# Score pairs inside dense weight units, fp32 units by token tile, gate columns on column quarters: one change to a fused two-block kernel

## The reference

```python
# first block
h = rms_norm(x, mix_norm_pre)
q, kc, vc, ksl, vsl, kw, vw, gt, pin, u, v = split(h @ w_in)      # 512, 6 x 128, 24, 256, 256, 256
gates = sigmoid(gt)                       # 8 heads x 3 branches
kc, vc = compress(kc), compress(vc)       # 15 compressed keys/values per group (2 groups of 4 heads)
# per 128-token block: three masked softmaxes (compressed, selected, window keys), each
#   gates[..., b] * (softmax(q k^T * 64**-0.5 + rel_bias) v)
x = x + rms_norm(concat(attention, pool_mixer(pin), sgu_mixer(u, v)) @ w_out)
x = x + rms_norm(memory_attention(rms_norm(x), rms_norm(mem), w_mq, w_mk, w_mv, w_mo))
x = x + rms_norm(conv_ffn(rms_norm(x), w_up, w_down))
# second block
proj = rms_norm(x) @ w_in_2               # qkv 1536, z 512, a 4, b 4, c_q, c_kv, k_idx, w_idx 4, ug 512
x = x + concat(gdn_mixer(...), dsa_mixer(...), conv_mixer(...)) @ w_out_2
x = x + cross_attention(rms_norm(x), mem_2)
x = x + relu(rms_norm(x) @ mlp_w1)**2 @ mlp_w2
```

## Time and profile before

| | |
|---|---|
| runs | 885.93 us median, 885.88 to 888.56 (n = 3) |
| profiled execution | 883.95 us, span 882.0 us |
| TensorE (PE) busy | 841.3 us, 95% |
| VectorE (DVE) busy | 558.8 us, 63% |
| ScalarE (ACT) busy | 406.0 us, 46% |
| granted TensorE clock, mean | 0.986 of full |
| DMA | 135.83 MB, 154 GB/s |

### The profile page before, as it was taken

One profiled execution on the slowest core, in us unless ns is written; L12 is line 12 of the kernel. 1 busy time (PEld: TensorE's weight loads), 2 busy tenths in 40 slices (PEclk: granted clock), 3 DMA queues, 4 the chain that ended last, 5 costly groups with the idle time before them and its releaser, 6 DMA issues.

```text
span 882.0 us, 14015 instructions
## 1 busy us (share of the span) xinstructions
PE 841.3 (95%) x5884; PEld 748.5 (85%) x5884; DVE 558.8 (63%) x808; ACT 406.0 (46%) x555; POOL 125.2 (14%) x163
## 2 busy tenths in 40 slices
PE   5998999999989999999999999999889899999998
PEld 5996877799879999999958898888668799999996
DVE  4448866628267876776675979974665665555552
ACT  4358442463235545544343565454434454444440
POOL 1134000210020000000021979510000000000000
PEclk9996999999999999999999899999999999999999
DMA  8974345362426655455414514201214196555521
GB/s 278 326 214 168 125 140 167 127 232 96 143 72 237 238 193 192 162 193 198 165 48 146 181 60 146 94 3 49 95 48 143 48 313 216 188 190 191 190 97 48
DMA packets 92346, 135.83 MB, mean 154 GB/s; under 512 B 4435, under 2 KB 76763, under 8 KB 92156
## 3 DMA queue, kind: packets, MB, share of 16 engines
q1 hardware_dynamic: 90428, 129.68, 44.2%
q0 software_dynamic: 736, 2.63, 0.9%
q10 hardware_dynamic: 1120, 2.62, 0.9%
HBM read 133.34 MB, written 1.06 MB: 152 GB/s over the span
## 4 chain that ended last, share of the span: by engine, by line
PE 82%; DVE 10%; ACT 3%; DMA 2%; issue 2%; POOL 1%; SPq 0%; POOLq 0%; DVEq 0%; ACTq 0%
PE work L2115 39%; PE acc L2115 24%; PE work L2071 2%; PE work L2092 2%; DVE split_extra_slot L1407 2%; PE work L2722 1%; PE work L2060 1%; DVE split_operands L1407 1%; DMA weight_ring<-in_w_up 1%; ACT hT L913 1%; PE work L2077 1%; PE work L2403 1%; DVE x_normed L1561 1%; PE work L2286 1%; PE work L2422 1%
## 5 line engine op out<-in xcount | busy, mean ns | idle before, releaser
L1407 DVE TENSOR_TENSOR split_operands<-weight_ring,split_operands 128x2048 fp32r<-128x2048 f32 x74 | 170.3, 2304 | 104.5 <-ACT split_operands L933 104.2
L2115 PE MATMUL work<-split_operands 128*128 128x256 f32 x1872 | 230.5, 284 | 1.3 <-DVE split_operands L1407 1.2
L2115 PEld LDWEIGHTS work<-split_operands 128*128 128x128 f32 x1872 | 227.6, 192 | 4.3 <-issue 3.1
L2115 PE MATMUL acc<-split_operands 128*128 128x512 f32 x840 | 197.5, 391 | 2.7 <-DVE split_operands L1534 1.4
L933 ACT ACTIVATE split_operands<-weight_ring 128x2048 fp32r<-128x2048 f32 x74 | 141.2, 1911 | 114.2 <-PE acc L2115 46.2
L2115 PEld LDWEIGHTS acc<-split_operands 128*128 128x128 f32 x840 | 156.0, 188 | 35.4 <-issue 2.3
L2115 PE MATMUL work<-split_operands,split_extra_slot 128*128 128x256 f32 x1056 | 131.8, 284 | 2.2 <-DVE split_extra_slot L1407 1.6
L2115 PEld LDWEIGHTS work<-split_operands,split_extra_slot 128*128 128x128 f32 x1056 | 129.1, 192 | 4.0 <-issue 2.3
L1407 DVE TENSOR_TENSOR split_extra_slot<-weight_ring,split_extra_slot 128x2048 fp32r<-128x2048 f32 x34 | 78.5, 2309 | 28.0 <-ACT split_extra_slot L933 27.7
L920 ACT ACTIVATE arena<-work 128x512 f32<-128x512 f32 (+1 forms) x65 | 35.7, 551 | 114.3 <-PE work L2115 76.7
L933 ACT ACTIVATE split_extra_slot<-weight_ring 128x2048 fp32r<-128x2048 f32 x34 | 64.8, 1907 | 26.2 <-PE acc L2115 11.6
(11 more groups left out here) (321 smaller groups left out, 899.3 us busy)
## 6 DMA issues: line engine op xcount, KB each, us to landing
weight_ring<-in_mlp_w SPq DMA_DIRECT2D x32, 1024.0 KB, 5.3
weight_ring<-in_w_up SPq DMA_DIRECT2D x22, 1024.0 KB, 5.1
weight_ring<-in_w_in SPq DMA_DIRECT2D x20, 1024.0 KB, 6.2
weight_ring<-in_w_down SPq DMA_DIRECT2D x11, 1024.0 KB, 4.9
weight_ring<-in_w_out SPq DMA_DIRECT2D x8, 1024.0 KB, 4.9
weight_ring<-in_w_mk SPq DMA_DIRECT2D x4, 1024.0 KB, 5.4
weight_ring<-in_w_mv SPq DMA_DIRECT2D x4, 1024.0 KB, 5.5
weight_ring<-in_w_mq SPq DMA_DIRECT2D x4, 1024.0 KB, 5.1
```

The source lines that it names most:

```text
L1407: dve.tensor_tensor(slot[:, 1, :], weights(split_units[i], 2048), slot[:, 0, :], ALU.subtract).then_inc(low_ready, 1)
L2115: ins = pe.matmul(out, lhs(p), rhs(q), start=(start and n == 0), stop=(stop and n == 2))
```

## The change

1. **Scores.** The 16 head scores leave the 4 work banks for the 4 acc banks. Four pairs of heads of t=0 and four of t=1 are issued two before `u`, two inside `u`, two inside `v`, two inside `mk 0` (after 5 and 11 of the unit's 16 steps). The transposes of the memory rows and the compression move ahead of `v`, and `cmp_h` inside it; the compressed scores come after `mk 0` and `mk 1`. VectorE's and ScalarE's orders follow. The split memory rows' high part lies in `xn` now, and the places of the input units are `(extra, 20480, 8704, extra, 20480, extra, 20480)`.
2. **Plain fp32 units by token tile.** `q0`, `xq 0` and `m1 0` become 32 products of 128 columns, those of t=0 first, each tile waiting only for its own rows.
3. **Fillers.** At `mem`, `ffn` and `mix2` a part of the plain unit that follows (4 of 16 steps, or 2 of 8) stands between the transposes of t=0 and t=1; VectorE scales and drains tile by tile.
4. **Gate columns.** `gates` and `ab` become 8 products with 32 weight columns each, on the four column quarters in turn, drained once, and summed with short products after `pool` and after `dk`.
5. **Output** in four DMAs of 256 KB in place of two of 512 KB.

```diff
-        phases = ((SPLIT_INPUTS, (None, 20480, 8704)), (("mk", "mv"), (None, 20480)),
+        phases = ((SPLIT_INPUTS, (None, 20480, 8704, None, 20480, None, 20480)), (("mk", "mv"), (None, 20480)),
...
-    fills = []
+    fills = [("s", t, h) for t in range(TT) for h in HEAD_ORDER]
...
             for t in range(TT):
-                sp.wait_ge(*acc_drained(("m2", 2 * t + 1)))
-                sp.dma_start(out[P * t:P * t + P, :], x[:, t, :]).then_inc(out_done, 16)
+                for half in range(2):
+                    sp.wait_ge(*acc_drained(("m2", 2 * t + half)))
+                    sp.dma_start(out[P * t:P * t + P, 512 * half:512 * half + 512], x[:, t, 512 * half:512 * half + 512]
+                                 ).then_inc(out_done, 16)
...
-            high_rows("memkv")
+            high_parts(upto(("mk", 0)))
             drain(("cmp_parts",), cmp_parts, bank(("cmp_parts",))[:, 0:2 * P].rearrange("p (v d) -> p v d", v=2)
                   ).then_inc(reader(("cmp_parts",)), 1)
+            high_rows("memkv")
...
+            for t in range(TT):
+                head_exps(t, 0, HEADS // 2)
+                high_parts(upto(("mv", 0)) + t)
+                drain(("mk", t), kmT[:, 2 * t:2 * t + 2, :], halves(("mk", t))).then_inc(reader(("mk", t)), 1)
+                head_exps(t, HEADS // 2, HEADS)
...
+            def norm_by_token_tile(stage):
...
+                for t in range(TT):
+                    dve.wait_ge(rstd_ready, STATI[(stage, t)] + 1)
+                    dve.tensor_scalar(xn[:, t, :], x[:, t, :], stat((stage, t)), None, ALU.mult).then_inc(normed, 1)
+                    for half in range(2):
...
+            def column_parts(name, unit):
+
+                ps = open_tile(name)
+                pe.wait_ge(*loaded(unit))
+                w = weights(unit, KD, 32)
                 for k in range(KD):
...
+                    q = k % 4
+                    ins = pe.matmul(ps[32 * q:32 * q + 32, 0:SEQ], w[:, k, :], hT[:, k, :], start=(k < 4), stop=(k >= KD - 4))
+                ins.then_inc(tile_full, 1)
...
+            def pair_by_token_tile(name, unit, stage):
...
+                for t in range(TT):
+                    rows_there(stage, t)
+                    for c in range(2):
+                        for k in range(KD):
+                            ins = pe.matmul(ps[:, SEQ * c + P * t:SEQ * c + P * t + P], w[:, k, P * c:P * c + P],
+                                            hT[:, k, P * t:P * t + P], start=(k == 0), stop=(k == KD - 1))
...
+            def norm_T_and_keys(stage, first, name, source):
+
+                rows_T(stage, first, 0)
+                ps = open_tile(name)
+                pe.wait_ge(*loaded(name))
+                mem_keys(ps, name, source, range(0, 4))
+                rows_T(stage, first, 1)
+                mem_keys(ps, name, source, range(4, 2 * KD)).then_inc(tile_full, 1)
...
+            for u in ("q0", "q1", "kskw", "vsvw"):
+                pe.wait_ge(*drained((u,)))
+            for i in range(2):
+                score_pair(0, i)
+            split_pair(("u",), "mix", "u", within_u)
+            norm_T("memkv", 2)
+            compress_blocks()
+            split_tall(("v",), "v", "mix", within_v)
+            compress_out()
+            rows_split("memkv")
+            split_pair(("mk", 0), "memkv", between=within_key)
+            compressed_heads(0)
+            split_pair(("mk", 1), "memkv")
+            compressed_heads(1)
```

More of the change, by code:

```diff
@@ L647, in stat @@
             return stats[:, c:c + 1]
-        hT_free = {"mix": None, "memkv": full(("gates",)), "mem": acc_filled(("mv", 3)), "mem2": acc_filled(("out", 3)), "ffn": full(("mk", 3)),
-                   "mix2": None, "cross": full(("abw",)), "mlp": full(("xq", 1))}
-        LAST_OF_UNIT = {u: full((u,)) for u in ("q0", "q1", "kcvc", "kskw", "vsvw", "gates", "pool", "u", "v")}
-        LAST_OF_UNIT.update({"cmp_w1k": full(("cmp_h",)), "cmp_w1v": full(("cmp_h",))})
+        hT_free = {"mix": None, "memkv": full(("gates_parts",)), "mem": acc_filled(("mv", 3)), "mem2": acc_filled(("out", 3)), "ffn": full(("mk", 3)),
+                   "mix2": None, "cross": full(("ab_parts",)), "mlp": full(("xq", 1))}
+        LAST_OF_UNIT = {u: full((u,)) for u in ("q0", "q1", "kcvc", "kskw", "vsvw", "pool", "u", "v")}
+        LAST_OF_UNIT["gates"] = full(("gates_parts",))
+        LAST_OF_UNIT.update({"cmp_w1k": full(("cmp_parts",)), "cmp_w1v": full(("cmp_parts",))})
         LAST_OF_UNIT.update({u: full(u) for u in units if u in TILE})
@@ L2147, in split_steps, with split_tall @@
                 return ins
[L2149 removed]
+            def split_tall(name, unit, stage, between=None):
                 ps = open_tile(name)
@@ new lines, in compress_blocks @@
+            def compress_blocks():
+                ps = open_tile(("cmp_parts",))
+                pe.wait_ge(blocks_ready, 1)
+                for kv, u in enumerate(("cmp_w1k", "cmp_w1v")):
+                    pe.wait_ge(*loaded(u))
+                    w = weights(u, CMP_PAIRS, P)
+                    for j in range(CMP_PAIRS):
+                        q = j % 4
+                        ins = pe.matmul(ps[32 * q:32 * q + 32, P * kv:P * kv + P], blocks[:, kv, j, :], w[:, j, :],
+                                        start=(j < 4), stop=(j >= CMP_PAIRS - 4))
+                ins.then_inc(tile_full, 1)
@@ new lines, in compress_hidden, with compress_out @@
+            def compress_hidden():
+                ps = open_tile(("cmp_h",))
+                pe.wait_ge(consts_in, 16)
+                pe.wait_ge(*drained(("cmp_parts",)))
+                for kv in range(2):
+                    ins = pe.matmul(ps[:, 32 * kv:32 * kv + 30], cmp_parts[:, kv, :], conc("sum_parts")[:, 0:30],
+                                    start=True, stop=True)
+                ins.then_inc(tile_full, 1)
+            def compress_out():
+                ps = open_tile(("cmp_kv",))
+                pe.wait_ge(*drained(("cmp_h",)))
+                w2 = parc("cmp_w2").rearrange("p (v d) -> p v d", v=2)
+                for g in range(GROUPS):
+                    pe.matmul(ps[DK * g:DK * g + DK, 0:NCMP], w2[:, 0, :], cmp_hT[:, 0, NCMP * g:NCMP * g + NCMP],
+                              start=True, stop=True)
+                for j in range(4):
+                    for g in range(GROUPS):
+                        ins = pe.matmul(ps[32 * j:32 * j + NCMP, 64 + DK * g:64 + DK * g + DK],
+                                        cmp_hT[:, 1, NCMP * g:NCMP * g + NCMP], w2[:, 1, :], start=True, stop=True)
+                ins.then_inc(tile_full, 1)
@@ L2277, in _, with compressed_heads @@
+            def compressed_heads(t):
+                pe.wait_ge(*drained(("cmp_kv",)))
                 for g in range(GROUPS):
```

358 lines of the change are left out of this document (177 added, 181 removed).

## The result

The changed kernel took 873.5 us (median of 4 runs, 871.56 to 875.2), the kernel before 887.17 (4 runs, 885.88 to 888.56): a ratio of 0.984 [0.981, 0.987] (in brackets, here and below, the 95% interval). The kernel before ran 11 times beside each group of experiments, at medians of 887.9, 887.7 and 887.8. So the change is worth 14.8 us.

A forecast was written before the change was run, and what follows sets the result against it. PE, busy 95% of the span, was taken to bound the kernel, with VectorE limiting scores to `mv`. Terms 6.6 + 1.9 + 2.4 + 1.2 + 0.5 = 12.6 us gave 873.3 us on the runs' scale; range 868.0 to 880.5, some 85%.

The forecast's parts named there:

- Part 1: Scores and compression, 43.6 to 124.0: `mv 3` ends at 117.4, gain 6.6 us; bounds 3.6 and 11.4.
- rivals 3 and 4: Scattered pairs cost what they save, 881, 5%; clock stays down through `v`, `mk 0` and `mk 1`, 889, 5%.
- rival 2: Gain mostly lost through longer waits, dearer turns and clock falls: 6 us less, 879.3, 22%.
- the fall behind `ga 1`: In rival 2, the clock falling once more at `ga 1`, priced by 0.9 us lost on transposes at `ffn`.
- the late split rows: In rival 2, ScalarE's late split rows making the waits of Part 1 3 us longer.
- `u` starts at 52.5, what `gates` and `q0` save is spent waiting for `u`: Start of `u` at 52.5 against 52.9 before, its weights landing at 47.79, delayed by DMA and not by PE.
- if VectorE's waits are filled, PE's list decides, 868.5: First rival, scores to `mv`: `mv` ends at 112.6, 4.8 us more gain, 868.5, 15%.
- Part 2: Plain units by token tile: waits go, doubled records cost 0.7 us each; gain 1.9 at `cross` and `mlp`.
- Part 3: Fillers before the second tile's transposes at `mem`, `ffn` and `mix2`: gain 2.4 us, bounds 1 and 2.7.
- Part 4: `ab`: PE 5.2 us shorter, 1.5 arrives, 4 us idle before `ga 1`; gain 1.2, bounds 0.3 and 5.2.
- Part 5: Output: last DMA carries 256 KB in place of 512; gain 0.5 us, bounds 0 and 1.3.

The follow-up runs named there:

- the kernel with the low parts shifted: Changed kernel, `mk 1`'s bank drained early and VectorE's low parts of `mv 1` to `mv 3` one step earlier: 868.85 us, 0.979 of the kernel before.
- part 1 alone: Kernel before with only the new scores, compression and `gates`: 881.75 us, 0.992 of the kernel before.
- taps first: Changed kernel with VectorE's row product and convolution taps of `qkv 1` ahead of the low part of `qkv 2`: 870.69 us.

## Why the prediction was right, and where it was not

**The number.** 873.3 for 873.5. But the gain was 14.8 us and not 12.6: the three runs of before that I had gave a median of 885.93, the 33 later ones 887.8. So two errors met, a low start and a low gain, and the hit to 0.2 us is luck; the terms are worth a look each.

**Part 1, forecast 6.6, alone 6.1.** The sum came out by the runs; by the traces 2.3 to 4.1 us of it stand before the end of `mv 3`, where the forecast had all. The steps were right only partly.
- Right: `mk 0` waits 1.28 us for its low part (forecast 1.0), `mv 1` waits 2.07 once nothing else is in the way (2.3), a pair of t=1 costs 1.06 from start to start (1.03), `u` with its two pairs ends 7.5 us after its start (7.5), so a pair and its turns cost (7.48 - 5.9) / 2 = 0.79 (0.84). No unit ran at half clock for long: rivals 3 and 4 fell. Of rival 2 the fall behind `ga 1` came, the late split rows did not.
- Wrong: "`u` starts at 52.5, what `gates` and `q0` save is spent waiting for `u`". It starts at 50.53, and its weights landed at 46.06 (the row below), 1.7 earlier than in the earlier trace rows. I had held a landing time fixed that was free to move. It moves with PE: in the thirteen traces ScalarE takes `u`'s weights 27.4 to 28.4 us after the unit behind `q0` starts, while that start itself lies between 18.02 and 20.97. That the ring's slots, freed earlier, are the link wasn't tried.

```profile
46.06 1.92 ACT L943 ACTIVATE split_extra_slot<-weight_ring 128x2048 fp32r<-128x2048 f32 x1 [8.95 <-DMA weight_ring<-in_w_in]
```

- Missed: the order that PE opens banks in. I followed queues on VectorE and ScalarE and never asked which tile the bank of `sgu_out` had held. The 2.15 us and the half clock behind them used up what `u` had won, and hid the wait at `mv 1` (0.24 in after).
- The step "if VectorE's waits are filled, PE's list decides, 868.5" came out as a time: the kernel with the low parts shifted took 868.85. Partly by luck: from the start of `gates` to the end of `mv 3` its trace takes 72.3 us, 1.55 of them waits, where the step had 69.4. The reason given against it, waits that are fixed by where PE issues the compressed scores, was wrong, since that kernel leaves those products where they are: PE's waits came of where VectorE's three low parts and one ScalarE drain stood.

**Part 2, forecast 1.9, undone 9.2.** This is the term that was mis-sized. In the traces the waits and the doubled records come out as I had them: 7.14 us from the first of 64 records to the next unit (7.5 taken), waits of 0.20. By the Trainium skill (TensorE: Matmul & The Clock Gate, the section on LDWEIGHTS) it would be 6.8, an estimate; the row lies midway between that and my value. The row doesn't say that the weight loads set it: half of a 256-column record of `xq 0` (32 in 6.8 us) gives the same 6.8 for 64. But I priced a wait of 1.7 us at 1.7 us. `xq 0` and `m1 0` had such a wait (1.39 to 1.70 us) in four traces: two of before, part 1 alone, no token tiles. At three of the eight places the clock fell behind it, and the unit took 1.4 to 3.0 us more: once in before, both times in the kernel without token tiles. And `q0`, put at nothing because its gain would be waited out at `u`, is worth up to 1.4 us: `u` was not waited for.

Why the kernel without token tiles loses 9.2 us by its times, and not the 4.9 at those two places, the granted clocks of all executions answer in part. Their mean is 0.986 over its six and 0.9915 over the eight of the changed kernel; times 875 us that is 4.8 us, an estimate of what half clock costs when nothing hides it. The two traces (0.984 and 0.988) differ by 3.5. With 2.4 us of waits and 1.1 in the first 20 us, less 0.7 for the doubled records, the 4.8 make 7.6; 1.6 us stay open.

**Part 3, forecast 2.4, undone 2.4.** Right in the sum; the traces show 0.3, 0.4 and 1.2 at the three places, where the terms were 0.4, 0.4 and 1.55.

**Part 4, forecast 1.2, undone 1.1.** The number is near, the working right only up to `ga 1`: PE 5.0 us shorter (5.2), 3.15 us idle before `ga 1` (4), then a fall of the clock. What was to arrive were the 1.49 us that VectorE waits in the earlier trace rows; in the kernel with the old columns that wait is 0.41, and by the traces nothing arrives. Nor did the fall cost what the term had: it took 2.4 us on `qkv 2`, but behind it PE would have waited for VectorE. That 1.1 meets 1.2 may be luck. I had taken VectorE's convolution for what sets this. The kernel with the taps first shows that the order behind it did: 2.3 us were to be had by moving one low part behind two other operations.

**Part 5, forecast 0.5, by the traces 0.6.** Right by the traces; the 2.1 of the runs is open.

**The parts don't add up.** Undone one at a time (part 1 by what it gives alone) they make 6.1 + 9.2 + 2.4 + 1.1 + 0.6 = 19.4 us (20.9 with the 2.1 of part 5's runs), against 14.8. The clocks on record show where much of the gain can lie. The mean over the 33 later executions of before is 0.9815, over the eight of the changed kernel 0.9915; what is missing to full clock, times the span, is 16.4 and 7.4 us. So up to 9.0 of the 14.8 us are clock, an estimate and an upper bound, since half clock that another engine's list hides costs nothing (`qkv 2`). The forecast counted clock at one place, the scores, and was worked out from a trace that was short of it by 12.3 us only. What a fall costs differs by what else is in the kernel; how the parts share the clock the runs don't show.

## What to carry to other kernels

When one wait is taken from a tight ring of engines, list what comes next at that place on every engine (bank, low part, drain) and move them together: here one fix gave 0.3 us, two gave 0.5, three gave 4.1. Ask of each new tile which tile its bank held and where that one's drain stands. Price a wait of TensorE by itself and by the unit behind it at half clock, and read that from several traces: a single one may show the fall or not. Then ask whether another engine's list hides it, as VectorE's did behind `ga 1`.

## What the runs showed of the hardware

- Whether the clock falls behind a wait differs from one execution to the next. Behind 1.61 us at `xq 0` it fell, behind 1.70 at the same place it did not; behind 2.82 us at `ffn` (the kernel with the old decay columns) it stayed up, behind 1.90 there (taps first) it fell. At the plain units a fall cost 1.4 to 3 us. The kernel with the old decay columns at `ffn`, its wait and the stretch behind it:

```profile
249.54 1.09 PE L2094 MATMUL work<-con,x_normed 128*128 128x128 f32 x8 [2.82 <-DVE x_normed L1399]
250.00:254.00 4.00, 3.65 (x24) 3.13 (x23) 2.50 (x4) 1.23 (x2) 0.86 (x2) 1.00 0.67 240
```

- Two products without use ahead of the transposes at `ffn` (1.88 us, in what was a wait of 1.7 to 3.6) were followed by no fall, in the one trace of it.
- Kernels whose first 20 us are the same differ there by 1.6 us from trace to trace: the unit behind `q0` starts at 18.02 to 19.66. The time lies in `q0` and the transposes before it (`q0` takes 7.31 to 8.56 us), at a granted clock that reads 1.00.
